# Rows picked straight from x in column pairs, one gate buffer for three branches, and four expert units loaded during the dense stage

## The chip, the cores and the metric

The kernel runs on one core of a Trainium2 chip. The metric is the time of the whole kernel on the device in microseconds (us). Before the change it is 702.25 us, the median of three runs (701.58 to 702.77).

## What is computed

One block of a language model on 256 tokens of width 1024, all in float32. First a root-mean-square norm and a wide projection, then three branches (a short convolution, an attention with a bias by distance, a gated linear attention), each with a sigmoid gate of its own:

```python
h = rms_norm(x, norm_mix)
merged = 0
for n, y_b in enumerate((y_conv, y_attn, y_gla)):
    merged = merged + sigmoid(h @ w_merge_gate[n]) * (y_b @ w_branch[n])
x = x + merged @ w_out
h2 = rms_norm(x, norm_ffn)
x = x + hier_moe(h2, ...)
```

`hier_moe` picks for each token one of 4 groups by a router, and in it the best two of 8 experts, so two of 32. For each expert the rows of `h2` that chose it are gathered, and

```python
y = (silu(xb @ w_gate[e]) * (xb @ w_up[e])) @ w_down[e]
```

is added to these tokens with its weight. `w_gate` and `w_up` are 1024 x 512 for each expert, `w_down` is 512 x 1024: 6 MiB for one expert, 192 MiB (201.3 MB) for all of them. All of it is read once, whatever the router chooses.

## The kernel before

There are two stages. The **dense stage** goes through 20 slots of dense weights of 2 MiB (`pre`): 9 for `w_in`, then for each of the three branches two halves of its gate and one branch product (slots 9 to 17), then two halves of `w_out` (18 and 19). They land in five ring slots (`ring`, `PRE_RING`), are split into a high part (`w_hi`, by ScalarE) and a low part (`ring_lo`, by VectorE), and TensorE does three products for each. `proj_done`, `chunk_done` and `branch_done` are the semaphores that tell how far that is.

The **expert stage** goes through the 32 experts. Its weights are cut into 192 units of 1 MiB: for each expert two of gate, two of up and two of down. They land in a ring of 22 places and one extra (`unit_at`, `RING`, `EXTRA`), which lie over tiles that the dense stage no longer needs by then. The first 23 units are loaded one by one by `first_load(n)`, each behind a wait for the last reader of what lay in its place; all later ones by `next_load`, mostly two units (2 MiB) in one transfer, behind `unit_free`, which TensorE raises when it is through with a unit. All these transfers stand in one queue, that of SyncE (SP), in the order in which the code issues them; a wait in that order holds back everything behind it.

Between the stages lies the **routing**. `out_quarter` adds the last columns of `merged @ w_out`, `x1_add` (L1886) adds them to `x_tok`, `turn_x1` (L1301) turns them, `x1T_out` copies them out, `route` (L1317) multiplies by the router's weights. VectorE finds the two experts of each token (`group_of`, `in_group`, `best_two`), and from them the selection matrix `pick_w` of the first expert (L1967). `seed` (L1310) puts `x_tok` into the four banks in which the result is summed.

For each expert TensorE multiplies `pick_w` with the normed rows (`pick_rows`, L1395), ScalarE copies the picked rows out (`xr`, L917), TensorE turns them (`turn_rows`, L1404), VectorE scales them (`xe`, L2040), and TensorE does gate and up (`gate_up`, L1431) and later down (`down`, L1468). The normed rows are two copies of `x_tok` times the reciprocal root `rstd`, with the columns put in another order: `xn2[0]` by GpSimd (L701) and `xn2[1]` by ScalarE (L904). They lie in 8 KiB of their own. The tile `x_tok` itself is the place of unit 20, which is therefore loaded only behind `seeded`, `xn0_ready` and `xn1_ready` (L563 to L565).

Once, ahead of expert 1, each of the engines waits for the number of passes (`route_ready`) and reads it into a register; TensorE also waits there for `table_ready` and `fold_ready` (L1535 to L1538).

## Time and profile before

| | |
|---|---|
| median of 3 runs | 702.25 us (701.58 to 702.77) |
| the profiled execution's own time | 701.26 us |
| its span, first to last instruction | 699.1 us |
| TensorE busy, share of the span | 615.8 us, 88% |
| VectorE, ScalarE, GpSimd busy | 40%, 29%, 4% |
| read from HBM | 245.72 MB |
| mean granted TensorE clock | 0.948 |

A row of a timeline gives the start and the length of an instruction (or of several alike), the engine, the line, what is written from what, and in brackets how long its engine had nothing to do before it and what ended that. A row of windows gives what each engine did in a stretch, then the granted clock, how busy the 16 DMA engines were and what they moved. The profile's own 701.26 us is 1.0 us below the median of the runs.

### The profile page before, as it was taken

The numbers are of one execution on the slowest core, as the hardware profiler recorded it, in microseconds if no ns is written. First come the engines' busy times: TensorE is split into PE (matmuls) and PEld (weight loads), VectorE is DVE, ScalarE is ACT, GpSimd is POOL, SyncE is SP. The second block draws the span as 40 slices with busy tenths as digits, with TensorE's granted clock in tenths as the row PEclk, the third lists the DMA queues.
The fourth block names the chain that finished last, engine by engine and source line by source line (L and its number), as shares of the span: only waits on it lengthen the run. The fifth ranks groups of instructions, "written<-read, shape, count | busy, mean of one in ns | idle before, by whom it ended". The sixth has DMA issues, their size and how long they took to land.

```text
span 699.1 us, 11551 instructions
## 1 busy us (share of the span) xinstructions
PE 615.8 (88%) x4690; PEld 373.8 (53%) x4690; DVE 279.8 (40%) x623; ACT 199.6 (29%) x334; POOL 28.5 (4%) x54
## 2 busy tenths in 40 slices
PE   8999999999999998999987788775878857797876
PEld 5887899999999893333332233322323323332333
DVE  6476976985474945333231112211112211120311
ACT  5684455473535433121111111111111111110111
POOL 2612000000000020000000000000000000000000
...
GB/s 314 309 373 185 133 139 221 155 133 229 166 272 420 304 387 398 428 424 426 429 426 427 429 427 427 427 425 427 428 427 429 425 428 427 428 425 429 426 419 211
DMA packets 40388, 247.53 MB, mean 354 GB/s; under 512 B 4456, under 2 KB 6640, under 8 KB 26128
## 3 DMA queue, kind: packets, MB, share of 16 engines
...
q14 instruction: 14, 0.11, 0.0%
HBM read 245.72 MB, written 1.06 MB: 353 GB/s over the span
## 4 chain that ended last, share of the span: by engine, by line
PE 57%; DMA 40%; DVE 1%; issue 1%; SPq 0%; POOL 0%; POOLq 0%; DVEq 0%
DMA wide<-in_w_expert_up 35%; PE ps L1431 9%; PE ps L1048 6%; PE ps L1049 6%; PE ps L1050 6%; DMA wide<-in_w_expert_down 5%; PE ps L1468 3%; PE ps L1023 3%; PE ps L1025 3%; PE ps L1024 3%; PE ps L1442 2%; PE ps L1524 2%; PE ps L1079 2%; PE ps L1395 1%; PE ps L1404 1%; PE ps L1091 1%
## 5 line engine op out<-in xcount | busy, mean ns | idle before, releaser
L1431 PE MATMUL ps<-wide,xe 128*32 128x512 f32 x1024 | 147.5, 700 | 72.0 <-DMA wide<-in_w_expert_up 70.2
L2083 DVE TENSOR_TENSOR he<-g_s,ps 128x128 f32<-128x128 f32 x32 | 9.2, 289 | 267.1 <-ACT g_s L935 264.2
L1431 PEld LDWEIGHTS ps<-wide,xe 128*32 128x32 f32 x1024 | 31.2, 119 | 145.0 <-issue 128.8
L1603 DVE TENSOR_TENSOR ring_lo<-ring,w_hi 128x1024 fp32r<-128x1024 f32 x76 | 91.3, 1222 | 41.4 <-ACT w_hi L742 41.0
L742 ACT ACTIVATE w_hi<-ring 128x1024 fp32r<-128x1024 f32 x76 | 78.9, 1057 | 54.8 <-PE ps L1050 34.9
L935 ACT ACTIVATE g_s<-ps 128x128 f32<-128x128 f32 x32 | 8.9, 277 | 252.1 <-PE ps L1442 252.1
L1048 PE MATMUL ps<-hT_hi,w_hi 128*128 128x256 f32 x288 | 80.4, 279 | 0.0
L1049 PE MATMUL ps<-hT_lo,w_hi 128*128 128x256 f32 x288 | 79.5, 276 | 0.0
L1050 PE MATMUL ps<-hT_hi,ring_lo 128*128 128x256 f32 x288 | 79.5, 276 | 0.0
L1524 PE MATMUL ps<-y,back 64*128 64x512 f32 x240 | 59.6, 611 | 1.9 <-ACT y L943 0.9
L1468 PE MATMUL ps<-wide,he 128*32 128x512 f32 x472 | 56.8, 598 | 0.0
L1442 PEld LDWEIGHTS ps<-fold,gu 128*128 128x128 f32 x256 | 36.4, 220 | 36.8 <-issue 36.8
L1048 PEld LDWEIGHTS ps<-hT_hi,w_hi 128*128 128x128 f32 x288 | 54.1, 188 | 0.3 <-issue 0.3
L1049 PEld LDWEIGHTS ps<-hT_lo,w_hi 128*128 128x128 f32 x288 | 54.1, 188 | 0.0
L1050 PEld LDWEIGHTS ps<-hT_hi,ring_lo 128*128 128x128 f32 x288 | 54.1, 188 | 0.0
L1442 PE MATMUL ps<-fold,gu 128*128 128x64 f32 x256 | 40.9, 310 | 0.0
L1524 PEld LDWEIGHTS ps<-y,back 64*128 64x128 f32 x240 | 23.3, 186 | 28.3 <-issue 28.3
L929 ACT ACTIVATE gu<-ps 128x512 f32<-128x512 f32 x32 | 19.1, 597 | 60.9 <-PE ps L1404 59.0
L2040 DVE TENSOR_TENSOR xe<-ps,g_ffn 128x256 f32<-128x256 f32 x32 | 13.6, 425 | 54.0 <-PE ps L1404 54.0
L943 ACT ACTIVATE y<-ps,w_slot 128x512 f32<-128x512 f32 (+1 forms) x31 | 21.1, 680 | 44.3 <-PE ps L1468 43.2
L1395 PE MATMUL ps<-xn,pick_w 128*32 128x256 f32 x512 | 33.5, 379 | 0.1
L1023 PE MATMUL ps<-w_hi,hT_hi 128*128 128x512 f32 x80 | 32.1, 402 | 0.0
...
## 6 DMA issues: line engine op xcount, KB each, us to landing
...
ring<-in_w_in SPq DMA_DIRECT2D x8, 2048.0 KB, 14.7
...
```

The lines of the kernel that those rows point to most:

```text
L742: s_.activation(by_row(w_hi[c]), piece(ring, g, c), ACT.Copy).then_inc(wpre_hi, 1)
L943: s_.activation(y[:, 0:width], bank(3)[:, 0:width], ACT.Copy, scale=w_slot[:, e % 2:e % 2 + 1]).then_inc(y_ready, 1)
L1023: t_.matmul(o, hT_hi[:, k, rows], by_row(w_hi[c])[:, j, :], start=(k == 0), stop=False)
L1048: t_.matmul(o, wh, x_hi[:, k, :], start=(k == 0 and j == 0), stop=False, skip_group_check=True)
L1049: t_.matmul(o, wh, x_lo[:, k, :], start=False, stop=False, skip_group_check=True)
L1050: ins = t_.matmul(o, wl[:, k - k0, cols_j], x_hi[:, k, :], start=False, stop=(k == nk - 1), skip_group_check=True)
L1395: ins = t_.matmul(ps[q * WIN:(q + 1) * WIN, e % 2, 0:QW], pick_w[e % 2][:, tt, :], xn2[tt][:, QW * q:QW * (q + 1)], start=(tt == 0), stop= ...
L1431: ins = t_.matmul(ps[q * WIN:(q + 1) * WIN, b, :], xe[b][:, j % 2, 2 * c + j // 2, :], w[:, C * j:C * (j + 1)], start=(c == 0 and j < 2), ...
L1442: ins = t_.matmul(bank(2, 8)[:, k, :], gu[:, k * P:(k + 1) * P], flat(fold[:, :, :]), start=True, stop=True)
L1468: ins = t_.matmul(ps[q * WIN:(q + 1) * WIN, 3, :], he[:, k, :], u[:, D * j + C * h:D * j + C * (h + 1)], start=(c == 0), stop=(c == 1))
L1524: t_.matmul(bank(4 + 2 * h + tt), back[e % 2][half, tt * P:(tt + 1) * P], y[half, :], start=False, stop=True, skip_group_check=True).then_ ...
L1603: v.tensor_tensor(piece(ring_lo, g, c), piece(ring, g, c), by_row(out_hi[g == 19][c]).bitcast(F32), ALU.subtract).then_inc(wpre_lo, 1)
```

## The change

- **Places in memory.** The scratch `scr` and the small tiles `w_al`, `zT`, `reset` now lie together in 8 KiB, and these are the place of unit 20. `x_tok` is no unit's place any more and lives to the end; the result is written into it (`fin`). The squares of the norm go to small scratch tiles.
- **No copies.** `xn2` is gone, and with it L701 and L904. `pick_rows` multiplies `pick_w` with `x_tok` itself. The four column groups of the picked rows are taken as column pairs: two neighbouring float32 of every eight. The copy to `xr` puts them in the order that the copies had before.
- **rstd goes into pick_w.** For the first expert one more small multiplication (`stat`, L1980), for all others the sum of the two selections becomes an instruction of its own (`join`), and `one_row` multiplies by `rstd`.
- **One gate buffer.** All three branches write their gate to `sig0`; that of branch 1 waits for the merge of branch 0, as that of branch 2 did for branch 1.
- **Loads.** Units 0, 1 and 2 are issued behind the dense slot 15 (they wait for the end of the attention, `pv_mm`), unit 11 behind slot 16. Unit 3 stays where it was. Unit 20 waits for `halves_squared` alone and is issued ahead of units 18, 17, 19, 21 and 22.
- **Order.** In the routing `turn_x1` and `route` of the last columns of the first 128 tokens come earlier on TensorE, and `in_group(0)`, `best_two(0)` come ahead of `x1_add(1, 2)` on VectorE. `eh` comes behind the first `pick_w`.
- **The number of passes** is read at expert 8 (`COUNT_AT`) instead of expert 1; TensorE waits for `table_ready` and `fold_ready` behind the first half of expert 1.

```diff
-        x_at = top[0]
+        scr_at = top[0]
+        scr = place("scr", [P, 2, C], F32)
+        w_al_at = top[0]
+        w_al = place("w_al", [P, 256], F32)
+        zT = place("zT", [P, T], F32)
+        top[0] += 1024
+        reset = place("reset", [P, T], F32)
+        xn_at = top[0]
+        assert xn_at - scr_at == 4 * UNIT
+        xn = place("xn_merged", [P, TT, D], F32)
         x_tok = place("x_tok", [P, TT, D], F32)
-        xn_at = top[0]
-        xn = place("xn_merged", [P, TT, D], F32)
...
-        xn2_at = (scr_at, w_al_at)
-        xn2 = [place(f"xn2_{tt}", [P, D], F32, at=at) for tt, at in enumerate(xn2_at)]
-        fin = [place(f"fin{tt}", [P, D], F32, at=at) for tt, at in enumerate(xn2_at)]
-        junk = [xn2[0], place("junk", [P, C], F32, at=w_al_at)]
+        fin = [x_tok[:, tt, :] for tt in range(TT)]
+        squares = [place("squares_half", [P, C], F32, at=scr_at)]
+        squares += [place("squares_quarter", [P, QW], F32, at=late_at)] * 2
...
-        unit_at += [ring_at[4], ring_at[4] + 4 * UNIT, gv_at, gv_at + 4 * UNIT, x_at, xn_at]
+        unit_at += [ring_at[4], ring_at[4] + 4 * UNIT, gv_at, gv_at + 4 * UNIT, scr_at, xn_at]
...
-                if n < 4 or n == 11:
+                if n < 3:
+                    sp.wait_ge(pv_mm, NH)
+                elif n == 11:
+                    sp.wait_ge(proj_done, first_bank[12])
+                elif n == 3:
                     sp.wait_ge(branch_done, 8)
                 elif n < 10:
...
+                elif n == 20:
+                    sp.wait_ge(halves_squared, 1)
+                else:
                     sp.wait_ge(proj_done, first_bank[NPRE - 2] + 6)
-                else:
-                    sp.wait_ge(seeded, 1)
-                    sp.wait_ge(xn0_ready, 1)
-                    sp.wait_ge(xn1_ready, 1)
...
-            for n in [0, 1, 2, 3, 11] + list(range(4, 11)) + [12, 14, 13, 15, 16, 18, 17, 19, 21, EXTRA, 20]:
+                if g == 15:
+                    for n in range(3):
+                        first_load(n)
+                if g == 16:
+                    first_load(11)
+            for n in list(range(3, 11)) + [12, 14, 13, 15, 16, 20, 18, 17, 19, 21, EXTRA]:
...
-            pool.wait_ge(rstd_ready, 1)
-            g.tensor_scalar(xn2[0][:, :].rearrange("p (k f) -> p k f", k=KD), x_tok[:, 0, :].rearrange("p (f k) -> p k f", k=KD),
-                            stat[:, 40:41], None, ALU.mult).then_inc(xn0_ready, 1)
...
-                if n == 2:
-
-                    act.wait_ge(branch_done, 2 * half + m + 1)
+                if n:
+
+                    act.wait_ge(branch_done, 4 * (n - 1) + 2 * half + m + 1)
                 dt = 4 * half + 2 * m
-                evac(9 + 3 * n + half, m, flat(sig[n][:, dt:dt + 2, :]), func=ACT.Sigmoid)
+                evac(9 + 3 * n + half, m, flat(sig0[:, dt:dt + 2, :]), func=ACT.Sigmoid)
...
-            x1T_out(1, 4, 6, 4)
-            x1T_out(0, 6, 8, 5)
+            x1T_out(0, 6, 8, 4)
+            x1T_out(1, 4, 6, 5)
             x1T_out(1, 6, 8, 6)
             x1_root(1)
-            act.wait_ge(proj_done, first_bank[NPRE - 2] + 6)
-            act.wait_ge(rstd_ready, 2)
-            s_.activation(xn2[1][:, :].rearrange("p (k f) -> p k f", k=KD), x_tok[:, 1, :].rearrange("p (f k) -> p k f", k=KD),
-                          ACT.Copy, scale=stat[:, 41:42]).then_inc(xn1_ready, 1)
...
-                s_.activation(xr[:, :], bank(e % 2)[:, 0:QW], ACT.Copy).then_inc(rows_out, 1)
+                s_.activation(xr[:, :].rearrange("p (k f) -> p k f", k=2), bank(e % 2)[:, 0:QW].rearrange("p (f k) -> p k f", k=2),
+                              ACT.Copy).then_inc(rows_out, 1)
```

```diff
+            def low_row(q, k):
+
+                return ring_lo[19 % PRE_RING][:, UNIT * q + QW * k:UNIT * q + QW * (k + 1)]
+
+            def out_begin(tt, q):
+
+                r = first_bank[19] + tt
+                if q == 0:
+                    pe.wait_ge(evacuated[r % 4], r // 4)
+                else:
+                    pe.wait_ge(x1_ready, tt + 1)
+
+            def out_quarter_low(tt, q, ks=range(KD)):
+
+                if ks[0] == 0:
+                    out_begin(tt, q)
+                for k in ks:
+                    ins = t_.matmul(bank(2 * q + tt)[:, 0:QW], merged_hi[:, k, tt * P:(tt + 1) * P], low_row(q, k),
+                                    start=(k == 0), stop=False)
+                if ks[-1] == KD - 1:
+                    ins.then_inc(chunk_done, 1)
...
-            out_quarter(1, 1, range(0, 2))
+            out_quarter_low(1, 1, range(0, 4))
+            turn_x1(0, range(6, KD), 5)
+            out_quarter_low(1, 1, range(4, KD))
             turn_x1(1, range(4, 6), 4)
-            turn_x1(0, range(6, KD), 5)
-            out_quarter(1, 1, range(2, 5))
-            route(0, range(6, KD), 5)
-            out_quarter(1, 1, range(5, KD))
-            route(1, range(4, 6), 4)
+            out_quarter(1, 1, range(0, 1))
+            route(0, range(6, KD), 4)
+            out_quarter(1, 1, range(1, KD))
+            route(1, range(4, 6), 5)
...
-                        ins = t_.matmul(ps[q * WIN:(q + 1) * WIN, e % 2, 0:QW], pick_w[e % 2][:, tt, :], xn2[tt][:, QW * q:QW * (q + 1)],
+                        rows_q = x_tok[:, tt, :].rearrange("p (f k) -> p f k", k=KD)[:, :, 2 * q:2 * q + 2]
+                        out_q = ps[q * WIN:(q + 1) * WIN, e % 2, 0:QW].rearrange("p (f k) -> p f k", k=2)
+                        ins = t_.matmul(out_q, pick_w[e % 2][:, tt, :], rows_q,
...
-            pe.wait_ge(xn0_ready, 1)
-            pe.wait_ge(xn1_ready, 1)
             pick_rows(0, 0)
             all_spots()
             turn_rows(0, 0)
             seed(1, 1)
-            seed(1, 3).then_inc(seeded, 1)
+            seed(1, 3)
...
-                pe.wait_ge(table_ready, 1)
-                pe.wait_ge(fold_ready, 1)
-                pe.wait_ge(route_ready, 1)
-                pe.reg_load(passes, npass[0:1, 0:1])
                 for e in range(1, NE - 1):
+                    if e == COUNT_AT:
+                        pe.wait_ge(route_ready, 1)
+                        pe.reg_load(passes, npass[0:1, 0:1])
                     gate_up(p, e, 0)
+                    if e == 1:
+                        pe.wait_ge(table_ready, 1)
+                        pe.wait_ge(fold_ready, 1)
...
+            v.engine_nop().then_inc(halves_squared, 1)
...
+            in_group(0)
+            best_two(0)
             x1_add(1, 2)
             square_sum(1, 2)
             mean_square(1)
-            in_group(0)
             scale_out(1)
-            best_two(0)
...
+            link(v.tensor_tensor(stat[:, 44:46], stat[:, 44:46], stat[:, 40:42], ALU.mult))
...
+            rstd = stat[:, 40:42].unsqueeze(2).broadcast_to([P, TT, WIN])
+
+            def join():
+
+                return v.tensor_tensor(same[:, :, 0, :], same[:, :, 0, :], same[:, :, 1, :], ALU.add)
+
             def one_row(dst):
 
-                return v.tensor_tensor(dst[:, :, :], same[:, :, 0, :], same[:, :, 1, :], ALU.add)
+                return v.tensor_tensor(dst[:, :, :], same[:, :, 0, :], rstd, ALU.mult)
...
+                join().then_inc(joined, 1)
+                dve.wait_ge(joined, i + (e + 1))
```

SyncE's queue from the dense slot 15 on, before. `ring` is a dense slot's weights, `wide` holds two units' places; the L539 rows are units 0, 1, 2, 3, 11 and 4 in this order.

```order
L578 DMA ring_49<-in_w_merge_gate 128x8x512 [waits proj_done]
L578 DMA ring_51<-in_w_merge_gate 128x8x512 [waits proj_done]
L578 DMA ring_53<-in_w_branch 128x4x1024 [waits proj_done]
L578 DMA ring_55<-in_w_out 128x8x512 [waits proj_done]
L575 DMA ring_57<-in_w_out 128x8x256 [waits proj_done]
L575 DMA ring_57<-in_w_out 128x8x256
L539 DMA wide_165<-in_w_expert_gate 128x2048 [waits branch_done]
L539 DMA wide_165<-in_w_expert_up 128x2048 [waits branch_done]
L539 DMA wide_166<-in_w_expert_gate 128x2048 [waits branch_done]
L539 DMA wide_166<-in_w_expert_up 128x2048 [waits branch_done]
L539 DMA wide_170<-in_w_expert_up 128x2048 [waits branch_done]
L539 DMA wide_167<-in_w_expert_gate 128x2048 [waits proj_done]
```

And now:

```order
L579 DMA ring_49<-in_w_merge_gate 128x8x512 [waits proj_done]
L538 DMA wide_161<-in_w_expert_gate 128x2048 [waits pv_mm]
L538 DMA wide_161<-in_w_expert_up 128x2048 [waits pv_mm]
L538 DMA wide_162<-in_w_expert_gate 128x2048 [waits pv_mm]
L579 DMA ring_51<-in_w_merge_gate 128x8x512 [waits proj_done]
L538 DMA wide_166<-in_w_expert_up 128x2048 [waits proj_done]
L579 DMA ring_53<-in_w_branch 128x4x1024 [waits proj_done]
L579 DMA ring_55<-in_w_out 128x8x512 [waits proj_done]
L576 DMA ring_57<-in_w_out 128x8x256 [waits proj_done]
L576 DMA ring_57<-in_w_out 128x8x256
L538 DMA wide_162<-in_w_expert_up 128x2048 [waits branch_done]
L538 DMA wide_163<-in_w_expert_gate 128x2048 [waits proj_done]
```

Units 0, 1, 2 (the first three L538 rows) stand behind the first gate slot of the last branch, unit 11 behind the second; the first unit behind the `w_out` slots is unit 3.

The end of that list before, from unit 16 (`wide_173<-in_w_expert_gate`) on. The last L539 row ahead of L537 is unit 20, and L537 is the first transfer into a place that an expert unit has left.

```order
L539 DMA wide_173<-in_w_expert_gate 128x2048 [waits chunk_done]
L539 DMA wide_174<-in_w_expert_gate 128x2048 [waits proj_done]
L539 DMA wide_173<-in_w_expert_up 128x2048 [waits chunk_done]
L539 DMA wide_174<-in_w_expert_up 128x2048 [waits proj_done]
L539 DMA wide_175<-in_w_expert_down 128x2048 [waits proj_done]
L539 DMA extra<-in_w_expert_down 128x2048 [waits proj_done]
L539 DMA wide_175<-in_w_expert_down 128x2048 [waits xn1_ready,xn0_ready,seeded]
L537 DMA wide_165<-in_w_expert_gate 128x4096 [waits unit_free]
L537 DMA wide_166<-in_w_expert_up 128x4096 [waits unit_free]
```

And now:

```order
L538 DMA wide_169<-in_w_expert_gate 128x2048 [waits chunk_done]
L538 DMA wide_171<-in_w_expert_down 128x2048 [waits halves_squared]
L538 DMA wide_170<-in_w_expert_gate 128x2048 [waits proj_done]
L538 DMA wide_169<-in_w_expert_up 128x2048 [waits chunk_done]
L538 DMA wide_170<-in_w_expert_up 128x2048 [waits proj_done]
L538 DMA wide_171<-in_w_expert_down 128x2048 [waits proj_done]
L538 DMA extra<-in_w_expert_down 128x2048 [waits proj_done]
L536 DMA wide_161<-in_w_expert_gate 128x4096 [waits unit_free]
L536 DMA wide_162<-in_w_expert_up 128x4096 [waits unit_free]
```

Unit 20 (`wide_171<-in_w_expert_down`, behind `halves_squared`) stands second, the extra unit last.

VectorE from the router's sums of the second 128 tokens to the first `pick_w`, before (`first` marks tokens of expert 0, `eh` is one-hot over the experts):

```order
L1920 MAX mg_91<-lg 128x8 [waits v_chain]
L1921 MAX_INDEX ig_92<-mg_91,lg 128x8 [waits v_chain]
L1925 TENSOR_TENSOR other<-iota_g,ig_92 128x32 [waits v_chain]
L1926 SCALAR_TENSOR_TENSOR le<-other,lg 128x32 [waits v_chain]
L1931 MAX me_93<-le 128x8 [waits v_chain]
L1932 MAX_INDEX ie_94<-me_93,le 128x8 [waits v_chain]
L1958 TENSOR_TENSOR first<-iota_f,ie_94 128x4 [waits v_chain]
L1961 TENSOR_TENSOR stat<-first 128x2 [waits assign_ready]
L1964 TENSOR_TENSOR eh<-iota_f,ie_94 128x128 [waits v_chain]
L1967 SCALAR_TENSOR_TENSOR pick_w_155<-iota_w,ps,stat 128x32 [waits pos_mm]
L1967 SCALAR_TENSOR_TENSOR pick_w_155<-iota_w,ps,stat 128x32
L1970 TENSOR_TENSOR below<-iota_f,ie_94 128x128
```

And now:

```order
L1937 MAX mg_92<-lg 128x8 [waits v_chain]
L1938 MAX_INDEX ig_93<-mg_92,lg 128x8 [waits v_chain]
L1942 TENSOR_TENSOR other<-iota_g,ig_93 128x32 [waits v_chain]
L1943 SCALAR_TENSOR_TENSOR le<-other,lg 128x32 [waits v_chain]
L1948 MAX me_94<-le 128x8 [waits v_chain]
L1949 MAX_INDEX ie_95<-me_94,le 128x8 [waits v_chain]
L1976 TENSOR_TENSOR first<-iota_f,ie_95 128x4 [waits v_chain]
L1979 TENSOR_TENSOR stat<-first 128x2 [waits assign_ready]
L1980 TENSOR_TENSOR stat<-stat 128x2 [waits v_chain]
L1985 SCALAR_TENSOR_TENSOR pick_w_151<-iota_w,ps,stat 128x32 [waits pos_mm,v_chain]
L1985 SCALAR_TENSOR_TENSOR pick_w_151<-iota_w,ps,stat 128x32
L1988 TENSOR_TENSOR eh<-iota_f,ie_95 128x128
```

The multiplication by `rstd` (L1980) is added, `eh` has gone behind `pick_w`.

## Rows read from the trace of the kernel before

**Rows 1.** The page, parts 1 and 2: busy time; GB/s in 40 slices of 17.5 us.
```profile
PE 615.8 (88%) x4690; PEld 373.8 (53%) x4690; DVE 279.8 (40%) x623; ACT 199.6 (29%) x334; POOL 28.5 (4%) x54
GB/s 314 309 373 185 133 139 221 155 133 229 166 272 420 304 387 398 428 424 426 429 426 427 429 427 427 427 425 427 428 427 429 425 428 427 428 425 429 426 419 211
```
**Rows 2.** Windows: length, busy PE, PEld, DVE, ACT, POOL, clock, DMA share, GB/s.
```profile
154.00:172.00 18.00, 18.00 (x160) 17.56 (x160) 12.22 (x14) 7.55 (x9) 0.00 (x0) 1.00 0.53 184
229.30:233.60 4.30, 4.30 (x33) 4.00 (x32) 4.26 (x6) 1.29 (x2) 0.00 (x0) 1.00 0.19 44
256.00:261.00 5.00, 4.75 (x37) 4.18 (x36) 2.65 (x14) 1.57 (x5) 3.29 (x1) 1.00 0.89 301
232.00:268.00 36.00, 35.19 (x259) 29.95 (x261) 23.34 (x70) 15.02 (x25) 3.98 (x1) 1.00 0.96 380
232.00:271.00 39.00, 38.19 (x295) 30.98 (x293) 25.86 (x85) 15.40 (x26) 3.98 (x1) 1.00 0.96 376
275.00:660.00 385.00, 318.34 (x2432) 122.59 (x2428) 84.88 (x261) 53.34 (x116) 0.00 (x0) 0.91 1.01 427
```
**Rows 3.** Timeline of SyncE's queue, the issues of transfers, 154 to 269 us.
```profile
154.91 12.44 SPq L578 DMA_DIRECT2D ring<-in_w_merge_gate  x2
...
201.74 0.35 SPq L539 DMA_DIRECT2D wide<-in_w_expert_gate  x1
...
203.07 0.90 SPq L539 DMA_DIRECT2D wide<-in_w_expert_up  x2
...
232.09 1.53 SPq L539 DMA_DIRECT2D wide<-in_w_expert_down  x2
...
247.33 2.22 SPq L539 DMA_DIRECT2D wide<-in_w_expert_gate  x2
255.83 3.20 SPq L539 DMA_DIRECT2D wide<-in_w_expert_up  x2
...
266.91 0.33 SPq L539 DMA_DIRECT2D wide<-in_w_expert_down  x1
268.82 0.33 SPq L537 DMA_DIRECT2D wide<-in_w_expert_gate  x1
```
**Rows 4.** Windows of 1 us about two gaps of the transfers; columns as above.
```profile
257.00:258.00 1.00, 1.00 (x10) 0.97 (x9) 0.00 (x1) 0.20 (x1) 1.00 (x1) 1.00 0.72 180
...
268.00:269.00 1.00, 1.00 (x19) 0.40 (x14) 0.86 (x5) 0.00 (x0) 0.00 (x0) 1.00 0.89 188
```
**Rows 5.** Timeline of TensorE from the last router product to expert 1.
```profile
260.17 0.64 PE L1317 MATMUL ps<-w_r,x1T 128*128 128x40 f32 x4
...
263.95 1.07 PE L1395 MATMUL ps<-xn,pick_w 128*32 128x256 f32 x16
...
266.81 1.92 PE L1431 MATMUL ps<-wide,xe 128*32 128x512 f32 x16
...
273.36 1.92 PE L1431 MATMUL ps<-wide,xe 128*32 128x512 f32 x16 [1.68 <-issue]
```
**Rows 6.** Timeline of VectorE in the routing.
```profile
245.27 0.08 DVE L1894 DVE_READ_ACCUMULATOR2_ANT stat<- 128x1 f32 x1
...
261.04 0.26 DVE L1918 SCALAR_TENSOR_TENSOR lg<-ps,stat,b_r 128x40 f32<-128x40 f32 x1
...
263.39 0.41 DVE L1967 SCALAR_TENSOR_TENSOR pick_w<-iota_w,ps,stat 128x32 f32<-128x32 f32 x2
...
268.53 0.23 DVE L2010 TENSOR_TENSOR pick_w<-same 128x64 f32<-128x64 f32 x1
```
**Rows 7.** Timeline of ScalarE, then of GpSimd: the two copies.
```profile
260.57 2.15 ACT L904 ACTIVATE xn<-x_tok,stat 128x1024 f32<-128x1024 f32 x1 [0.36 <-DVE stat L1912]
```
```profile
255.30 3.98 POOL L701 TENSOR_SCALAR xn<-x_tok,stat 128x1024 f32<-128x1024 f32 x1 [138.71 <-DVE stat L1912]
```
**Rows 8.** Weight loads by line, contiguous and strided: busy us, mean ns of one.
```profile
L1404 PEld LDWEIGHTS ps<-ident,xr 128*128 128x128 f32 x64 | 6.6, 144 | 28.6 <-issue 28.5
...
L994 PEld LDWEIGHTS ps<-ident,xn_merged 128*128 128x128 f32 x16 | 1.9, 193 | 0.5 <-issue 0.5
```
**Rows 9.** Timeline of TensorE: the first expert whose weights it waits for.
```profile
355.41 1.92 PE L1431 MATMUL ps<-wide,xe 128*32 128x512 f32 x16 [0.55 <-DMA wide<-in_w_expert_up]
```

64 lines of the change are left out of this document (26 added, 38 removed).

## The prediction

> **What bounds the kernel now.** I read the page first. TensorE is busy 88% of the span, which points at TensorE, but the line of GB/s says otherwise: from the slice at 280 us on it stands at 425 to 429 almost to the end [rows 1]. One row makes that exact: 427 GB/s over the 385 us from 275 to 660 [rows 2]. So the kernel has two halves. Up to 232 us TensorE works without a gap on the dense stage and the transfers have room: from 154 to 172 us they are at 184 GB/s [rows 2]. From about 270 us on the transfers are the bound and TensorE waits for them. A unit of 1 MiB takes 1.0486/0.427 = 2.46 us, an expert of six units 14.7 us. TensorE needs less: from expert 1 at 273.36 to the point where it has done eight more at 354.86 it takes 10.2 us for each, and it first waits for weights at 355.41 [rows 5, 9]. So 4.5 us of slack lie in each expert.
>
> The end is then set by one number: how many bytes of expert weights are still to come when the queue has become full for good. Only microseconds in which the transfers stand still, or more of them than before, move the end. The next view is therefore SyncE's queue [rows 3] beside what the transfers moved [rows 2, 4].
>
> Of the 23 units that fit, nine (0 to 7 and 11) are issued from 201.74 us on and have landed by 229.3. Then there is nothing to load: 229.3 to 233.6 has 44 GB/s [rows 2]. From 232.09 the other fourteen follow [rows 3]. From 232 to 268 the transfers moved 380 GB/s x 36 us = 13.68 MB, that is 13.05 units; from 232 to 271 it is 376 x 39 = 14.66 MB, or 13.98 units [rows 2]. So the fourteenth, unit 20, ends at 271.0. It was issued at 266.91, when ScalarE's copy was done; the first transfer of the reused places was issued at 268.82, when TensorE had left places 0 and 1 [rows 3], and its bytes follow unit 20's at 271.0 without a gap. From issue to first bytes it takes 1.7 us: the window from 268 holds 188/427 = 0.44 us of data, so data came back at 268.56, 1.65 us after 266.91; the window from 257 holds 0.42 us, 1.75 us after 255.83 [rows 3, 4].
>
> **Four units in the dense stage.** SP issues units 0, 1, 2 right behind the gate slot of 154.91 and unit 11 behind the next, at about 167. That adds 4 MiB, 9.8 us of transfer, into a stretch that is half empty [rows 2]. The slots behind them are five deep, so a delay of a few us is covered. But it moves nothing at the end. The same four units have landed before 229 now, and the queue runs dry at 229.3 for want of places. Units 8 and 9 wait for the last branch product and go at 232.09 in either version. Four units less between 201 and 226 us only make this dry time longer. Value: 0. The single gate buffer is what frees places 0 to 2; its new wait (ScalarE for the merge of branch 0) stands a whole gate half behind that merge, and only `high_pre` of a later slot is queued behind it. Value 0; up to 0.4 us if the wait shows.
>
> **Unit 20 early.** The squares of the first halves are done at 245.35 [rows 6], so `halves_squared` is up at about 245.5, and unit 20 goes right behind unit 16, issued at 247.33 [rows 3]. It fills a gap: from 256 to 261 the transfers were at 301, so 5 x (1 - 301/427) = 1.5 us were lost [rows 2], because unit 18 was through and unit 17 was issued at 255.83 only. Now the last of the 23 ends at 268.0 + 2.46 - 1.5 = 269.0 instead of 271.0. That would be 2.0 us, but the next bytes cannot come before TensorE frees a place. Call T the issue of that first reused place, 268.82 now. Bytes start at T + 1.7. With T unchanged this is 270.5, so 271.0 - 270.5 = 0.5 us is won and 1.5 us of new standstill appear from 269.0 to 270.5. Behind it there is no gap: 2 MiB last 4.9 us, and the second transfer comes one pick and one half of `gate_up` after the first, 3 us at most [rows 5]. **This is the term that decides: the end moves by 0.5 us plus whatever T moves.**
>
> **T.** The copies go, but they were not late. ScalarE's ended at 262.72, GpSimd's at 259.28 [rows 7], while `pick_w` was made from 263.39 to 263.8 and TensorE began to pick at 263.95 [rows 5, 6]. So removing them is worth 0 for T. The chain to T goes through the router: its last product ends at 260.81 [rows 5], VectorE takes it up at 261.04 [rows 6]. The span between holds the end of `best_two(0)`, which is now done earlier; at most 0.2 us, I take 0.1. `x1_add(1, 2)` waits for the last `out_quarter`, which the new order leaves at its place: the same matrix products stand ahead of it. The added product with `rstd` is hidden, since `pick_w` waits for TensorE's small products meanwhile. `eh` behind `pick_w` delays ScalarE's exponentials by about 0.1 us, and `xr` is copied behind these; I take nothing for it.
>
> Picking is the unknown. Sixteen products took 1.07 us from contiguous rows [rows 5]. Now each streams pairs, 8 bytes out of every 32. No row before streams such a pattern. The nearest is the weight load of L994, which takes one float32 of every eight: 193 ns against 144 for a contiguous one, x1.34 [rows 8]. Bounds: nothing, and 1.07 x 0.34 = 0.36 us; a gain has no source, since the same number of columns goes through. Half as many jumps as there speak for the lower part: 0.1 us. Together T stays: -0.1 + 0.1.
>
> On the same question the Trainium skill (SBUF — State Buffer, the note on cachelines under "Door 1: The DMA port swizzle") says that two hits in each 16-byte line are needed for full bandwidth, and that float32 can be strided by four for free. Pairs give just two hits in a line, but the stride is eight. By its first half picking costs nothing and the gain is 0.6; by its second it costs. No run here shows it yet.
>
> **Expert stage.** Slower picking by 0.1 to 0.4 us, and `join` on VectorE (0.23 us like the add of L2010 [rows 6], 31 times) lie in the 4.5 us of slack. ScalarE's strided copy likewise. Two joins ahead of `xe` of expert 1 cost 0.5 us on VectorE, which had about as much idle time there. Expert 1 can start some 1.2 us earlier, since the 1.68 us gap at 273.36 [rows 5] goes: worth 0, as the queue has 4 MiB before it by then. The read of the pass count at expert 8 costs TensorE up to 1.7 us, one expert ahead of 355.41; it is just before TensorE catches up with the transfers [rows 9], where all places are free and no transfer waits for it. Worth 0. The tail behind the last bytes has the same work.
>
> **Sum.** 701.26 - 0.5 = 700.8 by the profiled execution. That is 1.0 below the median of the runs, so against 702.25 it is 701.75; I write 701.7.
>
> **Rivals.**
> 1. *T comes clearly earlier.* If the routing shrinks by more than the rows show (ScalarE's 2.15 us are gone, GpSimd no longer reads beside VectorE), the gain grows one for one, until the bytes stand at 269.0: 2.0 us, time 700.2; with less lost at the start of the 14 units, up to 2.5, 699.7. For it: three engines are relieved in this stretch. Against it: TensorE waits for VectorE, whose rows are one chain. It decides from T = 267.9 on, where the gain passes 1.4 us.
> 2. *Early units count in full.* 4 x 2.46 = 9.8 us, 692.4. Against it stands the dry queue at 229.3 [rows 2]. For it only that the GB/s of the dense stage have room.
> 3. *Slower: pairs are read slowly.* If a line is fetched for each pair and the product takes three to four times as long, the first pick adds 2.1 to 3.2 us to T, and this is on the path: end +1.6 to +2.7, time 703.9 to 704.9. In the expert stage 10.2 + 3.2 = 13.4 us is still below 14.7, so it is paid once. It is slower than can be told apart from x2.8 on (1.9 us more for T). At x2 it is 702.8, no change. Against it: x1.34 in the nearest row [rows 8].
> 4. *The change does not do what it says*, unit 20 being held back by the transfers' order: then 270.9 and no gain, 702.25.
>
> **Chances.** About 0.2% of the time, 1.4 us, is what a measurement can tell from no change. Forecast with the fourth rival 0.66, all within 0.2%; rival 1 0.20, of which most is over 1.4 us; rival 2 0.03; rival 3 0.11, nearly all slower by over 1.4 us. That gives faster 0.22, same 0.67, slower 0.11. The forecast's own range is 700.9 to 702.4 (pick cost and T's 0.2, and 0.3 for the median of a few runs). Rival 1 reaches down to 699.7, the milder half of rival 3 up to 703: range 699.8 to 703.0.
>
> **What would show it.** In the new profile the dry time before 233.6 stays and begins earlier (217 to 221 us are nearly empty); 256 to 261 is at 420 or more; a new dip stands at 269 to 270.5, just ahead of the first reused place; T is within 0.3 us of 268.8; the 16 picks take 1.1 to 1.4 us; the row from 275 to 660 stays at 427. The prediction is wrong if T leaves 268.2 to 269.4, if the steady rate changes by half a per cent (2 us on the stream), or if unit 20 is not issued near 247.5.

## The result: slower by 0.23%, and what the profile after shows

The changed kernel takes 703.18 us (median of 22 runs, 702.44 to 705.25), the kernel before 701.66 us on the same chip (22 runs). The ratio is 1.0023, 95% interval 1.0018 to 1.0029, so the change costs 1.5 us. The forecast was 701.7 with a range of 699.8 to 703.0. It was counted from the median of three runs, 702.25; counted from the 22 runs its 0.5 us of gain would be 701.2, and the miss is 2.0 us. The profiled execution after took 702.97 us, 1.7 us more than that of before (701.26).

The page after, TensorE's busy time and the GB/s in 40 slices, which answer to [rows 1]:

```profile
PE 619.5 (88%) x4690; PEld 370.5 (53%) x4690; DVE 287.2 (41%) x655; ACT 197.5 (28%) x333; POOL 24.5 (3%) x53
GB/s 314 310 370 183 134 137 221 154 134 391 218 257 195 270 421 384 427 425 427 427 427 426 427 428 426 429 426 425 427 429 425 427 429 425 427 430 425 426 419 219
```

Windows after; the columns are those of [rows 2]:

```profile
154.00:172.00 18.00, 18.00 (x155) 17.56 (x154) 11.79 (x14) 7.80 (x9) 0.00 (x0) 1.00 0.85 325
...
229.30:233.60 4.30, 4.30 (x38) 4.30 (x38) 4.23 (x7) 3.25 (x4) 0.00 (x0) 1.00 0.31 130
256.00:261.00 5.00, 5.00 (x46) 5.00 (x45) 1.94 (x10) 2.03 (x4) 0.00 (x0) 1.00 1.02 421
232.00:268.00 36.00, 35.40 (x255) 31.30 (x253) 25.07 (x68) 13.82 (x24) 0.00 (x0) 1.00 0.89 363
232.00:271.00 39.00, 38.33 (x287) 33.05 (x289) 26.45 (x74) 14.56 (x26) 0.00 (x0) 1.00 0.90 368
275.00:660.00 385.00, 318.28 (x2424) 116.42 (x2428) 92.45 (x294) 54.57 (x117) 0.00 (x0) 0.92 1.01 427
```

The transfers do what was forecast: 154 to 172 us is fuller (184 to 325 GB/s), the gap from 256 to 261 is filled (301 to 421), the steady rate is the same 427. Only the nearly empty stretch that was forecast for 217 to 221 us came later, from 221 to 226 (43 GB/s). But look at the first row's count of products: 155 where [rows 2] had 160, in 18 us in which TensorE is busy throughout in both, at a granted clock of 1.00 in both. SyncE's queue after, for [rows 3], shows what that does:

```profile
155.18 0.55 SPq L579 DMA_DIRECT2D ring<-in_w_merge_gate  x1
156.01 0.41 SPq L538 DMA_DIRECT2D wide<-in_w_expert_gate  x1
...
167.49 0.55 SPq L579 DMA_DIRECT2D ring<-in_w_merge_gate  x1
...
235.33 0.95 SPq L538 DMA_DIRECT2D wide<-in_w_expert_down  x2
...
250.93 0.44 SPq L538 DMA_DIRECT2D wide<-in_w_expert_down  x1
...
259.28 2.89 SPq L538 DMA_DIRECT2D wide<-in_w_expert_up  x2
...
271.88 0.33 SPq L536 DMA_DIRECT2D wide<-in_w_expert_gate  x1
```

At 154.91 the two kernels are 0.27 us apart, at 232.09 they are 3.24 us apart (235.33), and T, the issue of the first reused place, goes from 268.82 to 271.88, 3.06 us later. So all of it is lost by the end of the last branch product. The cause stands in the durations. By tile, the durations (minimum, median, maximum in ns) of the products of two tiles, first before, then after:

```profile
L1048 PE MATMUL ps<-yc_hi,w_hi x32: 276/276/384, 155.6 to 166.3; 128*128 128x256 f32 x32
...
L1048 PE MATMUL ps<-hT_hi,w_hi x118: 276/276/276, 170.0 to 220.7; 128*128 128x256 f32 x118
```

```profile
L1048 PE MATMUL ps<-yc_hi,w_hi x32: 274/282/387, 155.9 to 167.0; 128*128 128x256 f32 x32
...
L1048 PE MATMUL ps<-hT_hi,w_hi x121: 281/281/281, 169.8 to 223.5; 128*128 128x256 f32 x121
```

From 155.6 to 232 us TensorE runs 672 products of 128x256, three for each block of weights. The first of them is followed by a gap, and the other 671 come without a break. The first and last starts of these, before:

```profile
155.84 0.28 PE L1049 MATMUL ps<-yc_lo,w_hi 128*128 128x256 f32 x1
...
231.79 0.28 PE L1050 MATMUL ps<-yg_hi,ring_lo 128*128 128x256 f32 x1
```

and after:

```profile
156.10 0.28 PE L1049 MATMUL ps<-yc_lo,w_hi 128*128 128x256 f32 x1
156.22 0.28 PE L1050 MATMUL ps<-yc_hi,ring_lo 128*128 128x256 f32 x1
...
235.02 0.28 PE L1050 MATMUL ps<-yg_hi,ring_lo 128*128 128x256 f32 x1
```

75.95 us over 670 steps is 113.4 ns a product, 78.92 us is 117.8. That is 2.97 us, with the same products in the same order. I call this the long stretch, and the mean distance from one product's start to the next its pace: 113.3 ns is the fast one, 117.8 ns the slow one (both without the first few products). Where the weights lie at 128 modulo 256, every stretch of such products in the traces is at one of the two, and most keep it from their first products to their end. Ten shorter stretches of 47 products between the blocks of the attention, 90 to 155 us, are at the fast pace in both kernels (113.4 to 113.6 ns with their first products).

The accounts close: the long stretch starts 0.26 later and takes 2.97 more, the routing takes 0.17 less (from 231.79 to 268.82, and from 235.02 to 271.88), together +3.06. The transfer of the results is issued at 694.63 us before and here after:

```profile
696.36 1.83 SPq L616 DMA_DIRECT2D out_x<-x_tok  x4
```

1.73 us later. So 1.3 us of the 3.06 came back. That this is what the rest of the change wins is shown below by d_yc, where the pace is restored and this transfer is issued 1.26 us earlier than before.

### The profile page after: what moved, and what is told of

Read it like the earlier page. It is cut to its first block, busy times and chain, and to the rows that moved or that the text cites. A ratio compares the mean times of both kernels' runs of the same rounds, so it can differ in the third digit from the quotient of the medians.

```text
span 700.9 us, 11583 instructions
## 1 busy us (share of the span) xinstructions
PE 619.5 (88%) x4690; PEld 370.5 (53%) x4690; DVE 287.2 (41%) x655; ACT 197.5 (28%) x333; POOL 24.5 (3%) x53
## 4 chain that ended last, share of the span: by engine, by line
PE 57%; DMA 39%; SPq 1%; DVE 1%; another core or an unknown queue 0%; issue 0%; POOL 0%; POOLq 0%; DVEq 0%
DMA wide<-in_w_expert_up 34%; PE ps L1446 8%; PE ps L1048 6%; PE ps L1049 6%; PE ps L1050 6%; DMA wide<-in_w_expert_down 5%; PE ps L1483 3%; PE ps L1023 3%; PE ps L1025 3%; PE ps L1024 3%; PE ps L1457 2%; PE ps L1539 2%; PE ps L1079 2%; PE ps L1412 1%; PE ps L1421 1%; PE ps L1091 1%
## 5 line engine op out<-in xcount | busy, mean ns | idle before, releaser
L1050 PE MATMUL ps<-hT_hi,ring_lo 128*128 128x256 f32 x288 | 80.2, 278 | 0.0
L1050 PEld LDWEIGHTS ps<-hT_hi,ring_lo 128*128 128x128 f32 x288 | 54.1, 188 | 0.0
L1412 PE MATMUL ps<-x_tok,pick_w 128*32 128x256 f32 x512 | 36.1, 397 | 0.0
L1539 PEld LDWEIGHTS ps<-y,back 64*128 64x128 f32 x240 | 20.7, 186 | 28.6 <-issue 28.6
```

Source lines behind the costliest of these rows:

```text
L1050: ins = t_.matmul(o, wl[:, k - k0, cols_j], x_hi[:, k, :], start=False, stop=(k == nk - 1), skip_group_check=True)
L1412: ins = t_.matmul(out_q, pick_w[e % 2][:, tt, :], rows_q, start=(tt == 0), stop=(tt == TT - 1))
L1539: t_.matmul(bank(4 + 2 * h + tt), back[e % 2][half, tt * P:(tt + 1) * P], y[half, :], start=False, stop=True, skip_group_check=True).then_ ...
```

## The experiments

Each time is the median of 5 to 12 runs, with the ratio to the kernel before on the same chip and its 95% interval. The groups ran on four chips, so two kernels of different groups are compared by these ratios. "T" is the issue of the first reused place; paces and T come from one profiled execution of each kernel.

### The loads, or the gate buffer?

The pace changes at the moment at which units 0 to 2 are issued (156.01), so the first theory, H1, blamed them; H2 blamed the one gate buffer, H3 the new places of the tiles. **a_late** is the changed kernel with its early loads taken back, **c_mid** has them behind slot 16, **b_early** is the kernel before with the early loads and the one gate buffer, **b_gate** has only the buffer.

```diff
 # a_late, against after
-                if n < 3:
-                    sp.wait_ge(pv_mm, NH)
-                elif n == 11:
-                    sp.wait_ge(proj_done, first_bank[12])
-                elif n == 3:
+                if n < 4 or n == 11:
                     sp.wait_ge(branch_done, 8)
...
-                if g == 15:
-                    for n in range(3):
-                        first_load(n)
-                if g == 16:
-                    first_load(11)
-            for n in list(range(3, 11)) + [12, 14, 13, 15, 16, 20, 18, 17, 19, 21, EXTRA]:
+            for n in [0, 1, 2, 3, 11] + list(range(4, 11)) + [12, 14, 13, 15, 16, 20, 18, 17, 19, 21, EXTRA]:
 # c_mid, against after
-                if g == 15:
-                    for n in range(3):
-                        first_load(n)
                 if g == 16:
-                    first_load(11)
+                    for n in (0, 1, 2, 11):
+                        first_load(n)
 # b_gate, against before; b_early has this and after's first_load of units 0 to 2, 3 and 11
-                if n == 2:
-                    act.wait_ge(branch_done, 2 * half + m + 1)
+                if n:
+                    act.wait_ge(branch_done, 4 * (n - 1) + 2 * half + m + 1)
...
-                evac(9 + 3 * n + half, m, flat(sig[n][:, dt:dt + 2, :]), func=ACT.Sigmoid)
+                evac(9 + 3 * n + half, m, flat(sig0[:, dt:dt + 2, :]), func=ACT.Sigmoid)
...
```

Expected of a_late:

> The changed kernel with its early loads taken back: units 0, 1, 2, 3 and 11 are again issued behind the last w_out slots, as before the change; unit 20 early, the single gate buffer, the pairs and the rest stay. Theory H1 (transfers issued at 156 us, where TensorE's stream restarts behind the attention, put the dense products on a slower pace that lasts): the 256-column products of 160 to 235 us stand 113.3 ns apart as in the kernel before, not 117.8 as after the change; the first reused place is issued at 268.6 (+-0.2) instead of 271.9; the time is 0.3 to 0.9 us below the kernel before, 700.8 to 701.3. Theories H2 (the single gate buffer) and H3 (the new places of the tiles) expect 117.8 ns, 271.9 us and 1.5 us above the kernel before, as after the change.

Expected of b_early:

> The kernel before with two parts of the change alone: the single gate buffer (which frees the places) and units 0, 1, 2 behind gate slot 15, unit 11 behind slot 16. Unit 20 stays late, the copies and the places of the tiles stay. H1 expects 117.8 ns between the dense products of 160 to 235 us, the first reused place at 272.0 instead of 268.8 and, since nothing is won by unit 20, an end 2.6 to 3.2 us later: 704.3 to 704.9 against 701.7. H2 expects 117.8 ns too. H3 (new places) expects 113.3 ns and a time within 0.3 us of the kernel before. What was recorded ahead of the result (early units are worth nothing) expects the time of before as well.

Expected of b_gate:

> The kernel before with the single gate buffer alone, all units at their old times. H1 and H3 expect 113.3 ns between the dense products, the first reused place at 268.8 (+-0.2) and the time of before within 0.3 us. H2 expects 117.8 ns and an end 2.6 to 3.2 us later.

Expected of c_mid:

> The changed kernel with all four early units behind slot 16 (issued near 167 us, in the middle of a gapless stretch of TensorE) and none behind slot 15 at 156 us, where the stream restarts. H1 in its narrow form (what counts is that transfers meet the restart) expects 113.3 ns from 156 to 235 us, the first reused place at 268.6 and 0.3 to 0.9 us below the kernel before. H1 in its wide form (any expert transfer beside the dense products slows them) expects 113.3 ns up to 167 us and 117.8 from there: about 2.6 us lost instead of 3.2, first reused place at 271.2, 1.0 us above the kernel before. H2 and H3 expect 117.8 ns from 156 us on and the time of the changed kernel.

Measured: a_late 702.88 us, 1.0013 (1.0004 to 1.0022), T 271.15, long stretch at 117.8 ns. c_mid 703.17, 1.0028 (1.0016 to 1.0040), T 271.94, 117.8 from 156 us on, ahead of any early load. b_early 701.52, 1.0000 (0.9991 to 1.0009), T 268.22, 113.3. b_gate 701.59, 0.9999 (0.9990 to 1.0008), T 268.76, 113.3. H1 and H2 fall: the pace goes neither with the loads nor with the buffer but with the family, slow in everything made from the changed kernel and fast in everything made from the one before. b_early and b_gate also show that early units and buffer are worth nothing, as forecast.

### An address, or a state?

What differs between the families ahead of 156 us is where tiles lie. H3a blames the place of `yc_hi`, H3b that of another tile; H4 takes the pace for a state into which a stretch falls. `yc_hi`, the input of the product at which the stretch starts, is placed at `scr_at`, a line that the diff leaves alone; but the change moves `scr` from the end of memory (223,808) to behind `w_hi` (114,816).

```diff
 # d_yc, against after
-        yc_hi = place("yc_hi", [P, KC, T], F32R, at=scr_at)
+        yc_hi = place("yc_hi", [P, KC, T], F32R, at=scr_at + 2496)
 # d_ycb, against before
+        yc_hi = place("yc_hi", [P, KC, T], F32R, at=w_al_at)
 # d_dup and d_brk, against after, ahead of the first product of slot g: (11, 1, T) and (13, 6, 64)
+                                if g == G and k == 0 and j == 0 and m == 0 and first == 0:
+                                    for _ in range(N):
+                                        t_.matmul(o[:, 0:COLS], wh, x_hi[:, k, 0:COLS], start=True, stop=False, skip_group_check=True)
```

Expected of d_yc:

> The changed kernel with one tile elsewhere: yc_hi, the input of the slot that starts at 156 us, 2,496 bytes further on in the same free room (its address modulo 4,096 is then what it was before the change; its own room moved with scr). So far each stretch of 128x256 products runs at one of two paces, 113.3 or 117.8 ns apart, from its first products to its end, and the long stretch from 156 us is slow in the three kernels with the new places and fast in the three with the old ones. H3a (the address of yc_hi, which the first products of the stretch read, decides): 113.3 ns from 156 to 232 us, the first reused place at 268.8 instead of 271.9, 0.3 to 1.2 us below the kernel before (700.5 to 701.4). H3b (another tile's new place decides: hT, yc_lo and the rest moved by 4,096 bytes): 117.8 ns and 1.5 us above the kernel before.

Expected of d_ycb:

> The kernel before with yc_hi alone moved, from scr's room at 223,808 to the room of w_al and zT at 132,512, free by then. H3a allows 117.8 ns (the first reused place at 271.9 and 2.6 to 3.2 us more time, 704.3 to 704.9) as well as 113.3, since this is a third address; 117.8 would show that the address of yc_hi is enough. H3b expects 113.3 ns, the first reused place at 268.8 and the time of before within 0.3 us.

Expected of d_dup:

> The changed kernel with the very first product of the stretch at 156 us issued twice (the second starts the sum anew, so nothing in the result changes): 0.12 us more work, all places as in the changed kernel. H4 (the pace is a state that the stretch falls into at its start and keeps, and any small change there may turn it): 113.3 ns and the first reused place at 269.0 is possible, time 700.7 to 701.6. H3 in the form that operands' addresses alone set the pace expects 117.8 ns and 0.1 us above the changed kernel, 703.3.

Expected of d_brk:

> The changed kernel with six short products (64 columns, each starts the same sum anew) ahead of slot 13, in the middle of the long stretch, near 178 us. H4 expects that the stretch after them can run at 113.3 ns although the same tiles are read, from 178 to 235 us: 2.2 us won against the changed kernel, 0.3 us spent on the six products, first reused place near 270.0, time 701.4 to 702.2. H3 (addresses of the tiles that are read) expects 117.8 ns on both sides of the break and 0.3 us more than the changed kernel.

Measured: **d_yc 699.89 us, 0.9976 (0.9967 to 0.9985)**, T 268.72, the long stretch at 113.3. One tile moved by 2,496 bytes gives 3.3 us and a kernel faster than both, 0.6 us below what was expected of it; unit 20 is the reason, as shown further down. d_ycb 702.06, 1.0005 (0.9996 to 1.0014), T 269.16. d_dup 703.23, 1.0020 (1.0011 to 1.0029), T 272.13, 117.8: one more product at the start does not turn the pace. d_brk 701.60, 0.9997 (0.9988 to 1.0006), T 270.45. TensorE's timeline in d_brk about the six short products (L1050):

```profile
177.92 0.28 PE L1051 MATMUL ps<-hT_hi,w_hi 128*128 128x256 f32 x1
...
178.27 0.28 PE L1051 MATMUL ps<-hT_hi,w_hi 128*128 128x256 f32 x1
...
178.63 0.75 PE L1050 MATMUL ps<-hT_hi,w_hi 128*128 128x64 f32 x6
179.21 0.36 PE L1051 MATMUL ps<-hT_hi,w_hi 128*128 128x256 f32 x1
...
179.64 0.28 PE L1051 MATMUL ps<-hT_hi,w_hi 128*128 128x256 f32 x1
...
179.98 0.28 PE L1051 MATMUL ps<-hT_hi,w_hi 128*128 128x256 f32 x1
```

Ahead of it a triple takes 0.35 us (177.92 to 178.27), behind it 0.34 to the end: 113.3 ns over 479 products. So H3a and H4 each hold a half. The address of `yc_hi` puts the stretch into the slow pace, and the pace is kept by products that read other tiles (`hT`, `ya`, `yg`), until something breaks the stream. In d_ycb it is not kept; by tile:

```profile
L1048 PE MATMUL ps<-yc_hi,w_hi x32: 277/278/384, 155.5 to 166.6; 128*128 128x256 f32 x32
...
L1048 PE MATMUL ps<-hT_hi,w_hi x125: 276/276/276, 168.0 to 221.0; 128*128 128x256 f32 x125
```

There the 96 products of the slot are at 117.8 ns and all later ones at 113.3.

### 64 bytes

The weights are loaded into TensorE, the other operand is streamed through it. In the fast kernels `yc_hi` lies at 64 modulo 256, like every other input that is streamed in the long stretch; the weights lie at 128. Theory A says that this remainder counts, theory B that the region does.

```diff
-        yc_hi = place("yc_hi", [P, KC, T], F32R, at=scr_at)
+        yc_hi = place("yc_hi", [P, KC, T], F32R, at=scr_at + OFFSET)
```

OFFSET is 2560, 64 and 192 on the changed kernel (e_2560, e_64, e_192), and 64 on the kernel before (f_b64).

Expected of e_2560:

> The changed kernel with yc_hi 2,560 bytes further on: 64 bytes beyond the place at which the long stretch ran at 113.3 ns, and at the same remainder modulo 256 (128) as in the changed kernel. The weights (w_hi, ring_lo) lie at 0 modulo 128; hT, yc_lo and all other inputs of the dense products at 64 modulo 128, and so did yc_hi in both kernels that were fast. Theory A (yc_hi must lie at 64 modulo 128 or 256; the line of bytes in which a row of it begins counts): 117.8 ns, the first reused place at 271.9, 703.2. Theory B (its region counts, 64 bytes make no difference): 113.3 ns, 268.8, 699.9.

Expected of e_64:

> The changed kernel with yc_hi 64 bytes further on: 192 modulo 256, 64 modulo 128. Theory A with 128: 113.3 ns, the first reused place at 268.8, 699.9. Theory A with 256, and theory B: 117.8 ns, 271.9, 703.2.

Expected of e_192:

> The changed kernel with yc_hi 192 bytes further on: 64 modulo 256 (320 modulo 512). Theory A with 128 or 256: 113.3 ns, the first reused place at 268.8, 699.9. Theory B, and a form of A that wants 64 modulo 512: 117.8 ns, 271.9, 703.2.

Expected of f_b64:

> The kernel before, nothing changed but yc_hi 64 bytes further on in its room: 128 modulo 256, 0 modulo 128. Theory A: 117.8 ns at least while the slot that reads yc_hi runs, from 156 to 167 us (0.4 us lost, the first reused place at 269.2, 702.1); if the pace also stays for the rest of the stretch, 3.1 us, 271.9 and 704.3 to 704.9. Theory B: 113.3 ns, 268.8 and the time of before.

Measured: e_2560 702.84, 1.0016 (1.0007 to 1.0025), T 271.59. e_64 703.01, 1.0019 (1.0010 to 1.0028), T 271.35. **e_192 699.64, 0.9969 (0.9957 to 0.9981)**, T 268.26, the lowest ratio of all. f_b64 704.59, 1.0042 (1.0027 to 1.0056). Against d_yc, e_2560 differs by 64 bytes and, by the ratios, 2.8 us. And f_b64 brings the loss into the kernel before with one number, 2.75 us (704.59 against 701.84); its products with `hT_hi`, and its T:

```profile
L1048 PE MATMUL ps<-hT_hi,w_hi x126: 281/281/281, 167.8 to 223.2; 128*128 128x256 f32 x126
```

```profile
271.80 0.33 SPq L537 DMA_DIRECT2D wide<-in_w_expert_gate  x1
```

Theory A with 256 holds so far (e_64 rules out 128), theory B falls.

### The terms of the forecast, and the weights' place

```diff
 # g_late20, against after with OFFSET 192
-            for n in list(range(3, 11)) + [12, 14, 13, 15, 16, 20, 18, 17, 19, 21, EXTRA]:
+            for n in list(range(3, 11)) + [12, 14, 13, 15, 16, 18, 17, 19, 21, EXTRA, 20]:
 # g_lateload: OFFSET 192 and a_late's loads
 # g_ring, against after
-    top = [16512]
+    top = [16704]
-        region = (top[0] + 191) // 512 * 512 + 320
+        region = (top[0] + 191) // 256 * 256 + 64
```

Expected of g_late20:

> The changed kernel with yc_hi at 64 modulo 256 (the version that took 699.6), and unit 20 issued last again, behind the extra unit, as before the change. The recorded forecast put 0.5 us on unit 20's early issue, limited by the first reused place; the version with the pace restored came out 1.8 to 2.2 us below the kernel before. If unit 20 carries all of it, this run is at 701.3 to 701.8, with the gap near 256 us back and unit 20's bytes ending near 271. If the rest of the change carries part of it (the later stretch of copies, the expert stage), it is between 699.9 and 701.2.

Expected of g_lateload:

> The version with the pace restored, and the early loads taken back: units 0, 1, 2, 3 and 11 behind the w_out slots. The recorded forecast (four units early are worth nothing, since the queue runs dry before 232 us all the same) expects 699.6 within 0.3 us and the first reused place at 268.3 to 268.8. If they carry part of the gain, it is 0.4 us or more above 699.6.

Expected of g_ring:

> The changed kernel with all tiles from the first ring slot to x_tok 192 bytes further on, and the region behind at the next place with 64 modulo 256: the weights (ring, w_hi), yc_hi, merged and x_tok go from 128 to 64 modulo 256, all others keep 64 modulo 256. Theory A-absolute (a tile that TensorE streams wants 64 modulo 256, whatever the weights' place): yc_hi is cured as in the last version, 113.3 ns, the first reused place at 268.5 or earlier, 699.6 or less; products that stream the weights (128x512 before 90 us, 229 ns apart; 128x256 at 243 us, 118 ns) may speed up too, up to 3 us in all. Theory A-relative (what counts is that the streamed tile and the loaded weights differ by 64 modulo 128 or by 192 modulo 256): with both at 64 all dense products run at the slow pace, 117.8 ns from 90 us on, first reused place at 272.5 or later, 703.5 or more.

Measured: g_late20 702.02, 1.0006 (0.9997 to 1.0015), T 268.70. g_lateload 699.57, 0.9975 (0.9967 to 0.9984), T 268.92. g_ring 706.99, 1.0080 (1.0066 to 1.0093), T 275.77. With unit 20 last the gain is gone: g_late20 takes by the ratios 2.1 to 2.6 us more than the three kernels that have it early (699.57 to 699.89), and 0.2 us more than was expected of it. The early units carry none of it. In g_late20 the gap is back although T is where d_yc has it:

```profile
256.00:261.00 5.00, 4.74 (x37) 4.20 (x36) 2.82 (x15) 1.69 (x5) 0.00 (x0) 1.00 0.88 293
```

The trace explains only a part of the 2.3 us. From 232 to 275 us g_late20 moves 381 GB/s and d_yc 390, which is 9 x 43/427 = 0.9 us. The profiled execution of g_late20 took 703.84 us, 1.8 above its median, and near its end the granted clock fell (the third number from the end, 0.50), while that of d_yc, below it, did not:

```profile
684.00:686.00 2.00, 2.00 (x16) 0.45 (x8) 0.00 (x0) 0.00 (x0) 0.00 (x0) 0.50 0.85 343
```

```profile
684.00:686.00 2.00, 1.71 (x24) 1.07 (x22) 0.00 (x0) 0.28 (x1) 0.00 (x0) 1.00 0.74 299
```

Whether the other executions have this too is not known, so about 1.4 us of what unit 20's issue is worth stay without a place in the trace.

g_ring put weights and inputs both at 64 modulo 256. By tile:

```profile
L1048 PE MATMUL ps<-hT_hi,w_hi x128: 283/283/283, 169.9 to 227.1; 128*128 128x256 f32 x128
```

All its 128x256 stretches run at 119.7 to 120.0 ns, slower than any in the other kernels. So it is not the address of the streamed tile alone that counts: the same tiles at the same remainder are slow once the weights move. I read this as a distance between the two. That the weights want a remainder of their own, whatever the streamed tile's, would fit as well; no run moved both together. (Its 128x512 products before 90 us gained a little, from 230.5 to 227.6 ns on average against after.)

### Which distances?

The same edit of `yc_hi` on the changed kernel, OFFSET 128 (h_128) and 224 (h_224).

Expected of h_128:

> The changed kernel with yc_hi 128 bytes further on: 0 modulo 256, that is 128 away from the weights (which lie at 128 modulo 256). So far a streamed tile 192 bytes after the weights (modulo 256) is fast, and 0, 32 and 64 are slow. Theory A-relative, half (what counts is another 128-byte half than the weights', so 128 to 255 are fast): 113.3 ns, the first reused place near 268.5, 699.7. Theory A-relative, narrow (only 192 is fast): 117.8 ns while yc_hi is read at least, 702 to 703.

Expected of h_224:

> The changed kernel with yc_hi 224 bytes further on: 96 modulo 256, that is 224 after the weights. Half: 113.3 ns, 699.7. Narrow: 117.8 ns while yc_hi is read at least; the pace may fall back to 113.3 afterwards, as it did at a distance of 32: 700.1 to 703.

Measured: h_128 700.11, 0.9979 (0.9969 to 0.9989), T 269.09; h_224 702.69, 1.0018 (1.0008 to 1.0028), T 271.58. "Narrow" holds for the pace while `yc_hi` is read; the time that it gave for h_128, 702 to 703, missed, because the pace fell back behind the slot. The six places seen, with the weights at 128. The pace is that of the 96 products that read `yc_hi` or `yc_lo`, without the first four, and of the 576 behind them:

| `yc_hi` modulo 256 | distance from the weights | pace while it is read, ns | pace of the rest, ns |
|---|---|---|---|
| 64 (before, d_yc, e_192) | 192 | 113.3 | 113.3 |
| 0 (h_128) | 128 | 117.8 | 113.3 |
| 160 (d_ycb) | 32 | 117.8 | 113.3 |
| 128 (after, e_2560, f_b64) | 0 | 117.8 | 117.8 |
| 192 (e_64) | 64 | 117.8 | 117.8 |
| 96 (h_224) | 224 | 117.8 | 117.8 |

The 117.8 is a mean over three products, and its parts depend on the place. Between the three starts of a block the traces have medians of 113, 120 and 120 ns in d_ycb, 120, 117 and 117 in h_128, 120, 114 and 119 in h_224, 118, 114 and 122 in e_64; each adds up to about 353 ns, where the fast pace has 340. In g_ring all three are 120.

One stretch does not fit the table. The first one of the dense stage, from 10.8 to 21.9 us, streams `hT`, which lies at the good distance of 192 in both kernels, and yet runs at 117.8 ns in both. In e_192 it runs at 113.4. Its products before, and in e_192:

```profile
L1079 PE MATMUL ps<-hT_hi,w_hi x32: 281/281/364, 10.6 to 20.0; 128*128 128x256 f32 x32
```

```profile
L1079 PE MATMUL ps<-hT_hi,w_hi x32: 276/276/369, 10.4 to 19.5; 128*128 128x256 f32 x32
```

The changed kernel and e_192 have the same places and the same products up to there, so something other than the places decides here, and a distance of 192 allows the fast pace without securing it. At 94 steps this is 0.4 us.

What stays open: all other tiles streamed in the long stretch kept 64 modulo 256, so outside g_ring the table can as well be read as "`yc_hi` must lie like its neighbour in the stream, `yc_lo`". Why 0 and 160 let the pace fall back and 96, 128 and 192 do not was not found, and by what mechanism the places act at all is not shown.

## Why the prediction was wrong, point by point

**"Up to 232 us TensorE works without a gap on the dense stage", "T unchanged".** This is the step that failed. No gap was taken to mean that nothing in that stage could move. But a stage in which TensorE is busy all the time is one in which 4.4 ns a product go straight to T: 670 times, 2.97 us. The change's only touch on it was `scr`, whose move was read as bookkeeping; every tile of `region` had been kept at 64 modulo 256, and `yc_hi`, riding on `scr_at`, lost it. The warning signs named in the text did show: T left 268.2 to 269.4 and unit 20 was issued at 250.93, not near 247.5. No rival had this mechanism; "slower" had 0.11, all of it on slow pairs.

**"Four units in the dense stage: value 0", "the gate buffer: 0".** Right: b_early and b_gate are at 1.0000 and 0.9999, and g_lateload (0.9975) is within the noise of e_192 (0.9969).

**"Unit 20 early: 0.5 us".** The mechanism was right, the size was not. With the pace restored the windows of d_yc are

```profile
232.00:271.00 39.00, 38.32 (x296) 30.90 (x294) 26.29 (x86) 13.32 (x25) 0.00 (x0) 1.00 0.96 386
256.00:261.00 5.00, 4.73 (x37) 4.19 (x36) 2.82 (x15) 1.68 (x5) 0.00 (x0) 1.00 1.02 423
...
268.00:269.00 1.00, 1.00 (x20) 0.47 (x16) 0.86 (x5) 0.00 (x0) 0.00 (x0) 1.00 0.91 369
269.00:270.00 1.00, 1.00 (x20) 0.42 (x16) 0.83 (x6) 0.38 (x1) 0.00 (x0) 1.00 1.07 279
270.00:271.00 1.00, 1.00 (x12) 0.13 (x4) 0.83 (x7) 0.00 (x1) 0.00 (x0) 1.00 0.54 172
```

The gap at 256 is gone and the new dip stands where it was forecast, but it loses (58 + 148 + 255)/427 = 1.08 us instead of 1.5. And "its bytes follow unit 20's at 271.0 without a gap" was wrong of the kernel before. Its window there, and that of d_yc behind it:

```profile
272.00:275.00 3.00, 1.64 (x16) 0.50 (x16) 2.62 (x9) 1.66 (x2) 0.00 (x0) 1.00 0.93 350
```

```profile
272.00:275.00 3.00, 2.85 (x24) 1.39 (x24) 2.57 (x9) 1.61 (x2) 0.00 (x0) 1.00 1.01 431
```

That was a second hole of 3 x (427 - 350)/427 = 0.54 us, which no row of the forecast looked at and which goes with the first. The sum becomes 0.5 + 0.42 + 0.54 = 1.5 us; the transfer of the results is issued at 693.37 in d_yc, 1.26 us before that of the kernel before (in e_192 1.97), and the medians say 1.8 to 2.2. So this term was worth three times what was written, 1.5 us by the trace and 2.3 by g_late20, of which the rest is not explained. With the pace restored the kernel does come out clearly faster, by 1.8 us in d_yc.

**"T: -0.1 + 0.1".** Right within 0.2: from the last product of the long stretch to T it is 0.17 us less than before. VectorE and TensorE after, for [rows 5, 6]:

```profile
264.09 0.26 DVE L1935 SCALAR_TENSOR_TENSOR lg<-ps,stat,b_r 128x40 f32<-128x40 f32 x1 [0.52 <-PE ps L1330]
...
266.47 0.42 DVE L1985 SCALAR_TENSOR_TENSOR pick_w<-iota_w,ps,stat 128x32 f32<-128x32 f32 x2
```

```profile
263.33 0.64 PE L1330 MATMUL ps<-w_r,x1T 128*128 128x40 f32 x4
...
266.95 1.13 PE L1412 MATMUL ps<-x_tok,pick_w 128*32 128x256 f32 x16
...
275.33 1.92 PE L1446 MATMUL ps<-wide,xe 128*32 128x512 f32 x16 [0.52 <-DVE xe L2068]
```

VectorE starts 0.12 us behind the last router product instead of 0.23, its chain to `pick_w` takes 2.38 instead of 2.35, and the sixteen picks take 1.13 instead of 1.07. Expert 1 starts 3.45 us behind T instead of 4.54, 1.1 earlier where 1.2 was forecast, and waits 0.52 us for `xe`. The copies were not late, as forecast. In d_yc, with the same start of routing within 0.07 us, T is 268.72.

**"Pairs are read slowly", rival 3.** It fell: the picks from pairs cost 0.06 us, less than the 0.1 taken. By the note of the Trainium skill cited in the forecast (SBUF — State Buffer, under "Door 1: The DMA port swizzle") two hits in a line are enough; the trace agrees with that half, and the stride of eight did no harm.

**Rivals 1, 2, 4.** T came earlier than 268.7 only where the long stretch itself began earlier (b_early, e_192: by 0.6 us and 0.4), both with the first stretch of the kernel at the fast pace; the early units do not count; unit 20 was not held back.

**Expert stage: 0.** Right: 427 GB/s in [rows 2] and after, with 33 more instructions of VectorE from 275 to 660 us.
